# Gate/up weights in two pieces of 4 MB per expert in place of four of 2 MB

## What is computed

```python
logits = h @ router_w + router_b
top_val, top_idx = lax.top_k(logits, 4)          # 4 of 32 experts for each of 256 tokens
gates = softmax(top_val)
# for each expert e, on the tokens that chose it:
gu = xb @ w_gate_up[e] + b_gate_up[e]            # w_gate_up: 32 x 1024 x 2048
gate = minimum(gu[:, :1024], 7.0); up = clip(gu[:, 1024:], -7.0, 7.0)
y = ((up + 1.0) * gate * sigmoid(1.702 * gate)) @ w_down[e] + b_down[e]   # w_down: 32 x 1024 x 1024
```

## Time and profile before

| | |
|---|---|
| median of 3 runs | 1090.15 us (1087.44 to 1090.32) |
| profiled execution, device time | 1088.34 us |
| its span, first to last instruction | 1086.6 us |
| PE busy | 989.3 us, 91% |
| DMA | 423.99 MB, mean 390 GB/s over the span |
| TensorE's granted clock, mean | 0.986 of full |

### The profile page before, as it was taken

How to read it: one execution, slowest core, us unless ns; L and a number is a source line. 1 busy time by engine, 2 the same in 40 slices (tenths; PEclk the granted TensorE clock), 3 DMA queues, 4 the chain that set the end, 5 groups by cost and what they waited for, 6 DMA issues and landing times.

```text
span 1086.6 us, 12110 instructions
## 1 busy us (share of the span) xinstructions
PE 989.3 (91%) x4624; PEld 419.8 (39%) x4624; DVE 208.9 (19%) x445; ACT 158.1 (15%) x281; POOL 42.8 (4%) x138
## 2 busy tenths in 40 slices
PE   7999969999999999999898888888989989888887
PEld 4446644434343434333333333333333333333333
DVE  1047153211111111111111111111111111101112
ACT  2235140110101010101010101010010101010100
POOL 0250000000000000000000000000000000000000
PEclk9999978999999999999999999999999999999999
DMA  9669935999999999999999999999999999999995
GB/s 310 191 163 376 346 130 210 425 429 427 417 397 426 431 426 428 430 426 430 428 429 430 426 429 428 429 429 426 430 428 429 429 426 430 427 429 429 426 431 217
DMA packets 40697, 423.99 MB, mean 390 GB/s; under 512 B 6199, under 2 KB 8397, under 8 KB 16013
## 3 DMA queue, kind: packets, MB, share of 16 engines
q1 hardware_dynamic: 38728, 422.59, 93.9%
q10 hardware_dynamic: 1956, 1.25, 0.5%
HBM read 421.20 MB, written 2.62 MB: 390 GB/s over the span
## 4 chain that ended last, share of the span: by engine, by line
DMA 52%; PE 44%; DVE 2%; ACT 1%; issue 1%; SPq 0%; ACTq 0%; DVEq 0%
DMA dring<-in_w_down_dram 46%; PE bank L742 15%; PE bank L711 13%; PE bank L511 6%; DMA ring<-in_w_gate_up_dram 3%; PE bank L666 2%; PE bank L673 2%; DMA mt<-in_b_gate_up_dram 1%; PE bank L552 1%; PE bank L519 1%; DMA ring<-in_w_in_dram 1%; PE bank L625 1%; DVE mt L1041 1%; ACT mt L852 1%; PE bank L614 0%
## 5 line engine op out<-in xcount | busy, mean ns | idle before, releaser
L711 PE MATMUL bank<-ring,mt 128*64 128x512 f32 x2048 | 455.1, 593 | 6.8 <-DMA ring<-in_w_gate_up_dram 5.0
L742 PE MATMUL bank<-dring,mt 128*64 128x512 f32 x1024 | 237.3, 612 | 69.8 <-DMA dring<-in_w_down_dram 59.9
L711 PEld LDWEIGHTS bank<-ring,mt 128*64 128x64 f32 x2048 | 146.7, 137 | 291.1 <-issue 261.8
L1157 DVE TENSOR_SCALAR mt<-bank 128x512 f32<-128x512 f32 x32 | 22.1, 692 | 729.9 <-PE bank L711 729.9
L742 PEld LDWEIGHTS bank<-dring,mt 128*64 128x64 f32 x1024 | 71.5, 139 | 215.0 <-issue 133.0
L891 ACT ACTIVATE mt<-mt 128x512 f32<-128x512 f32 x32 | 20.1, 630 | 429.7 <-DVE mt L1157 429.7
L899 ACT ACTIVATE short<-bank 64x512 f32<-64x512 f32 x64 | 37.9, 592 | 284.3 <-PE bank L742 283.9
L666 PEld LDWEIGHTS bank<-mt,hn 128*128 128x128 f32 x544 | 64.2, 197 | 14.1 <-issue 13.0
L666 PE MATMUL bank<-mt,hn 128*128 128x128 f32 x544 | 67.9, 284 | 1.0 <-DVE st L1084 1.0
L673 PE MATMUL bank<-short,mt 128*128 128x512 f32 x136 | 62.9, 605 | 1.3 <-ACT short L899 1.3
L511 PE MATMUL bank<-ring,mt 128*128 128x512 f32 x128 | 58.1, 609 | 1.7 <-DMA ring<-in_w_in_dram 1.7
(11 more groups left out here) (171 smaller groups left out, 392.4 us busy)
## 6 DMA issues: line engine op xcount, KB each, us to landing
ring<-in_w_gate_up_dram SPq DMA_DIRECT2D x128, 2048.0 KB, 32.8
dring<-in_w_down_dram SPq DMA_DIRECT2D x64, 2048.0 KB, 25.3
ring<-in_w_in_dram SPq DMA_DIRECT2D x4, 1024.0 KB, 12.1
ring<-in_w_in_dram SPq DMA_DIRECT2D x2, 2048.0 KB, 19.7
dring<-in_w_out_dram SPq DMA_DIRECT2D x2, 2048.0 KB, 25.5
dram_bias<-ring SPq DMA_DIRECT2D x1, 1536.0 KB
xs<-in_x_dram SPq DMA_DIRECT2D x2, 512.0 KB, 4.9
mt<-in_w_kv_b_dram SPq DMA_DIRECT2D x1, 1024.0 KB, 12.8
```

The costliest lines, as they stand in the source:

```text
L711: last = nc.tensor.matmul(ps[64 * h:64 * h + 64, :], xeT[:, k, b * SLOT:(b + 1) * SLOT], GU[b][:, k, u * FF + h * HALF:u * FF + (h + 1) * ...
L742: last = nc.tensor.matmul(ps_a[64 * h:64 * h + 64, :], hT[:, o:o + SLOT], DN[:, c * 4 + k, h * HALF:(h + 1) * HALF], start=c == 0 and k == ...
L1157: V.tensor_scalar(g_sb, ps_gate[:, :], LIMIT, None, ALU.min).then_inc(gate_ready, 1)
```

## The change

Each expert's gate/up weights are loaded in two pieces of 4 MB, with 32 KB consecutive per partition.

```diff
-NCHUNK, DCHUNK = 4, 2
+NCHUNK, DCHUNK = 2, 2
```

## The result

| | before | after |
|---|---|---|
| median of 4 runs | 1090.24 us (1087.44 to 1091.52) | 1098.74 us (1098.34 to 1099.38) |
| profiled execution, device time | 1088.34 us | 1098.90 us |
| its span | 1086.6 us | 1097.1 us |

The ratio after to before is 1.0082 (95% interval 1.007 to 1.0094): slower by 8.5 us in the medians, by 10.6 us between the two profiled executions.

The account below looks back on a forecast made before the run. DMA at 429 GB/s was taken to set the end, with PE fed just in time after 430 us. Start and order +4.9, tail +3.4, longer runs -3.9, biases +5.3 made +9.7 on 1088.3: 1098.0 us, range 1091.5 to 1103.5.

Parts of the forecast that it names:

- Start of the steady loading: SP's first loop loads: a 4 MB piece is released later, so data flows 3.5 us later, not added separately.
- Where the queue runs dry: SP's in-order load queue: later start and changed order leave DMA dry longer before down 5, together +4.9 us.
- Longer runs: Loop loads of experts 6 to 31: each 32 KB run replacing two of 16 KB saves 9.5 ns, -3.9 us taken.
- rival 2: Gate/up loads: hardware moves 32 KB runs as two of 16 KB, nothing saved, +8.3 us, 1096.6; chance 0.15.
- Rival 4: Loads after 302 us: each DMA has a price, 52 fewer make it faster, 1029 at 1.4 us each; chance 0.05.
- The tail: End of kernel: PE has 32 matmul records after the last gate/up piece lands instead of 16, +3.4 us.
- The biases' load: Prologue: ACT's gate/up bias load takes turns with SP's longer runs and lands later, delaying expert 0 by 5.3 us.
- rival 1: Prologue: the biases land as before, leaving +4.4 us, 1092.7; chance 0.18.
- rival 3: Prologue: the biases are held back by all of SP's queued runs, +4.4 + 10.3 us, 1103.0; chance 0.08.
- Rival 5: Whole kernel: no change, saving at upper bound, order at +1.8, biases not delayed, about +0.5 us, 1088.8; chance 0.09.

Follow-up runs that it names:

- a_loophalf: The kernel after, with each 4 MB gate/up piece in the loop loaded as two 2 MB DMAs with 16 KB runs: 1102.54 us, ratio 1.0123 to before.
- a_prohalf: The kernel after, with only the prologue's four 4 MB gate/up loads each issued as two of 2 MB with 16 KB runs: 1094.65 us, ratio 1.0049 to before.
- a_order: The kernel after, with one gate/up piece again issued ahead of the wait for down in SP's loop: 1094.24 us, ratio 1.0046 to before.
- b_order: The kernel before, with down issued ahead of all four 2 MB gate/up pieces in SP's loop: 1094.36 us, ratio 1.0048 to before.

## Why the prediction came out right, step by step

**Start of the steady loading: +3.5, taken in by the next step.** SP's first issue of the loop came 7.12 us after PE's first gate/up matmul (183.43 less 176.31), against 3.69 before. Right.

**Where the queue runs dry: +4.9.** One dry stretch, 4.7 us from about 302, was forecast at 4 to 5 us, 126 to 130 us after expert 0's start. That the order is its cause was argued then and is shown now: taking the order out gave back 4.5 us by the medians and brought the end of the loads 4.7 us forward, putting it into the kernel before cost 5.2.

**Longer runs: -3.9.** The runs did move as single packets of 32 KB (rival 2 falls by the packet count), and undoing them in the loop cost 3.8 us by the medians, 4.5 by the ratios and 4.4 up to the last piece in the profile. The fixed 9.5 ns per run, taken from runs of 2 and 16 KB, held at 32 KB within this scatter (4.4 us would be 10.6 ns). Rival 4, a price for each DMA, falls with it: it needed at least 0.22 us for each, and 0.01 is left.

These terms as forecast and the measured 4.5 us by which expert 0 was late give the place of the last piece: 4.5 + 4.9 - 4.0 = 5.4 us later, as measured.

**The tail: +3.4, measured +5.1.** This term was too small. What the prediction had in it is right: in a_loophalf, whose last 32 records run at full clock (7.09 us), it is 12.3 us from the last piece to the down matmuls (1072.84 to 1085.15) in place of 8.9, +3.4. But in the kernel after the matmuls of the last 4 MB took 8.78 us. PE had waited 2.18 us for the piece, and the window over it shows what it was granted:

```profile
1066.00:1078.00 12.00, 10.18 (x45) 4.08 (x46) 1.29 (x2) 0.62 (x1) 0.24 (x1) 0.86 0.83 352
```

With a clock of 0.86 there (0.50, the lower level, from 1069 to 1071) the remaining 1.7 us are accounted for. That the wait lowers it is only the order in which the two appear. In the kernel after PE waited 2.2 us for a second piece 14 times: ten times its 32 records then took 8.64 to 8.79 us, four times 7.09. After the 17 shorter waits for gate/up, of at most 1.2 us, they always took 7.09. Why four of the long waits did not do it stays open. So whether the last piece is hit is partly luck: in a_loophalf PE waited 2.27 us for it and it was not. The prediction had looked for PE's wait of 2.3 us at the second piece and had put nothing on what it does to the clock.

**The biases' load: +5.3, measured +3.2 in this profile.** This term was too large. ACT waited 19.0 us, not 21. Its direction and cause hold: rival 1 (no effect) falls by the wait itself, rival 3 (the amount queued) by a_prohalf, in which the amount is the same and the wait 14.0 us. The figure had counted one turn of 0.89 us more for each of six bias runs. Two more kernels have the prologue of the kernel after: from its issue the biases' load took 18.7 us to land there, 19.7 in a_order and 19.5 in a_loophalf, against 15.3 in the kernel before and 15.2 in b_order. So the effect is 3.4 to 4.5 us over these executions. Between a_prohalf (13.7) and the kernel after, whose prologues differ in nothing but run length, it is 5.0; so the size of a turn is right to within the scatter, and the wait of before also held something that the new placement took away. What that is was not settled. The Trainium skill (DMA: Bandwidth & Descriptors, Queues, rings and completion order) says that a DMA engine takes turns between queue rows by whole packets. The runs agree in kind: with longer runs in SP's queue the other queue's load landed later; the turns themselves are in no view.

Expert 0 began 4.5 us later, not 5.3: 3.2 from the biases, and 1.1 because this execution was behind already when the biases' load was issued (118.81 against 117.75), which is scatter: that issue lies between 117.0 and 118.8 over the profiled executions with and without the change.

So the sum, +9.7 against a measured +8.5 in the medians and +10.6 in the profiles, is right with two errors that offset one another, the tail 1.7 us too small and the biases 1 to 2 us too large. The terms were forecast to within 2 us each; that the sum is closer than that is luck. Rival 5 (no change) needed the order to cost 1.8; it cost 3.9 to 5.2.

## What to carry to other kernels

When a buffer is refilled in fewer, larger pieces, look at what else the piece count decides: here `NCHUNK // 4` became 0, which moved a load behind a wait on an in-order queue and cost more than the larger transfers saved. Price a larger transfer on its own by its runs (here 9.5 ns for each run that disappears) and hold against it the last piece, which the consumer can only begin when it has all landed. And where a small load on the critical path meets bulk loads that have time, let the bulk wait for it: one added wait was worth 9.4 us in the kernel before and 12.3 us in the kernel after, more than any other edit of this study.

## What the runs showed that was not expected

- An idle PE costs more than its idle time. After 7.0 us of waiting, 12 transposes took 2.82 us at a granted clock of 0.50; without the wait they took 1.60 us at 1.00.
- Ten of 14 waits of 2.2 us before a 4 MB piece were followed by 32 matmul records that took 8.6 to 8.8 us in place of 7.1. After none of 17 shorter waits was that so.
- Splitting SP's runs from 32 to 16 KB shortened another queue's wait from 19.0 to 14.0 us with the same bytes queued.
